# Splitting an expert's weights by halves over two engines in a two-block transformer kernel

## What is computed

```python
g_val, g_idx = lax.top_k(softmax(t @ w_group + b_group), 1)      # 1 of 4 groups
e_val, e_idx = lax.top_k(softmax(e_logits[group]), 2)            # 2 of its 8 experts
...
hid = silu(einsum('td,edf->tef', t, w1)) * einsum('td,edf->tef', t, w3)
hid = hid * combine[:, :, None]
y = einsum('tef,efd->td', hid, w2)
```

## Time and profile before

| what | value |
|---|---|
| median of 3 runs | 2845.2 us (2840.59 to 2852.76) |
| the profiled execution, its own time | 2848.42 us |
| its span, first to last instruction | 2846.7 us |
| busy: TensorE matmul, weight load | 90%, 70% |
| busy: VectorE, ScalarE, GpSimd | 62%, 34%, 53% |
| DMA moved | 386.72 MB, mean 136 GB/s |
| chain that ended last | TensorE 30%, GpSimd 20%, issue 19%, VectorE 14%, DMA 12%, ScalarE 3% |

### The profile page before, as it was taken

The page is one execution under the profiler, slowest core; times in us unless marked ns, Lnnn a source line. Parts: engine busy times, 40 slices in busy tenths (PEclk is TensorE's granted clock), DMA queues, the critical chain, the costliest instruction groups (busy, mean ns, idle before and its releaser), DMA issues.

```text
span 2846.7 us, 36510 instructions
## 1 busy us (share of the span) xinstructions
PE 2563.7 (90%) x12750; PEld 2006.6 (70%) x12750; DVE 1772.8 (62%) x2113; ACT 954.8 (34%) x1416; POOL 1515.9 (53%) x1234
## 2 busy tenths in 40 slices
PE   4977989968999999899598889999995879999998
PEld 3754767856777777678377348888884768888887
DVE  6769855647677776556688665666234964666314
ACT  2013256733443432567422222222013631222102
POOL 4730344526444453445366106767777847666775
PEclk8977889989999999899899679999997999999999
DMA  8746468952332322688522112333231113333222
GB/s 308 256 133 207 171 243 307 315 176 81 96 93 85 103 78 96 248 316 317 178 64 92 48 52 78 99 99 89 96 115 59 34 45 100 92 100 97 88 96 82
DMA packets 319121, 386.72 MB, mean 136 GB/s; under 512 B 51579, under 2 KB 259215, under 8 KB 318903
## 3 DMA queue, kind: packets, MB, share of 16 engines
q1 hardware_dynamic: 261424, 335.84, 35.8%
q10 hardware_dynamic: 34438, 28.08, 3.2%
q0 software_dynamic: 23168, 21.59, 2.4%
HBM read 397.62 MB, written 55.41 MB: 159 GB/s over the span
## 4 chain that ended last, share of the span: by engine, by line
PE 30%; POOL 20%; issue 19%; DVE 14%; DMA 12%; ACT 3%; SPq 1%; ACTq 0%; POOLq 0%; DVEq 0%
POOL WL L830 14%; PE PAIR L528 6%; PE PAIR L529 5%; PE PAIR L530 5%; POOL WH L826 5%; DMA RAW<-in_moe_w 4%; DMA RAW<-in_ffn_w_up 3%; PE PAIR L1831 2%; PE BANK L2261 2%; PE BANK L528 1%; PE BANK L529 1%; PE BANK L530 1%; DVE WL L1933 1%; DVE ADA_SUM L633 1%; PE PAIR L1801 1%
## 5 line engine op out<-in xcount | busy, mean ns | idle before, releaser
L830 POOL TENSOR_TENSOR WL<-RAW,WH 128x512 fp32r<-128x512 f32 x584 | 819.2, 1432 | 12.2
L528 PE MATMUL PAIR<-HH,WH 128*128 128x512 f32 x1792 | 713.2, 398 | 50.1 <-POOL HL L1119 29.1
L529 PE MATMUL PAIR<-HL,WH 128*128 128x512 f32 x1792 | 703.7, 393 | 0.0
L530 PE MATMUL PAIR<-HH,WL 128*128 128x512 f32 x1792 | 702.8, 392 | 0.0
L825 POOL TENSOR_TENSOR TURN<-ONES 128x1 f32<-128x1 f32 x146 | 34.3, 235 | 938.7 <-PE PAIR L530 860.5
L528 PEld LDWEIGHTS PAIR<-HH,WH 128*128 128x128 f32 x1792 | 340.3, 190 | 134.8 <-issue 45.7
L529 PEld LDWEIGHTS PAIR<-HL,WH 128*128 128x128 f32 x1792 | 340.4, 190 | 71.6 <-issue 2.4
L530 PEld LDWEIGHTS PAIR<-HH,WL 128*128 128x128 f32 x1792 | 340.1, 190 | 71.8
L826 POOL TENSOR_SCALAR WH<-RAW 128x2048 fp32r<-128x2048 f32 x146 | 281.5, 1928 | 0.0
L1933 DVE TENSOR_TENSOR WL<-RAW,WH 128x2048 fp32r<-128x2048 f32 x78 | 178.6, 2292 | 151.2 <-ACT WH L1751 135.7
L2003 POOL DMA_INDIRECT XG<-htok_scratch,GATHER_I x78 | 148.0, 1897 | 213.1 <-PE PAIR L1801 131.3
(11 more groups left out here) (523 smaller groups left out, 4649.2 us busy)
## 6 DMA issues: line engine op xcount, KB each, us to landing
RAW<-in_moe_w SPq DMA_DIRECT2D x156, 512.0 KB
RAW<-in_ffn_w_up SPq DMA_DIRECT2D x88, 512.0 KB
W2RAW<-in_moe_w SPq DMA_DIRECT2D x78, 512.0 KB
ADA_B<-in_ada_w SPq DMA_DIRECT2D x30, 1024.0 KB, 5.4
RAW<-in_ssm_w_in SPq DMA_DIRECT2D x48, 512.0 KB
ADA_A<-in_ada_w SPq DMA_DIRECT2D x18, 1024.0 KB, 7.7
RAW<-in_ffn_w_down SPq DMA_DIRECT2D x32, 512.0 KB
RAW<-in_ev_w_in SPq DMA_DIRECT2D x20, 512.0 KB
```

What stands on the lines that cost most here:

```text
L528: nc.tensor.matmul(o, wh, xh, start=start, stop=False)
L529: nc.tensor.matmul(o, wh, xl, start=False, stop=False)
L530: return nc.tensor.matmul(o, wl, xh, start=False, stop=stop)
L830: ins = pool.tensor_tensor(WL[:, s, c], RAW[:, s, c], WH[:, s, c].bitcast(F32), ALU.subtract)
```

## The change

A slot's unit is now handled in halves. w1 and w3 are loaded by two transfers with a semaphore each: w1 counts on the new `w1_landed`, w3 alone on `landed` (so the wait counts of all later units change: `landed_count`). ScalarE makes WH in two instructions of 1024 columns: the first when w1 has landed, signalling the new `w1_hi`, the second when w3 has landed, signalling `split_hi`. VectorE makes WL of the first half and signals the new `w1_low`. GpSimd makes WL of the second half in one instruction of 1024 columns (`second`) and signals `split_ready`. `second(0)` stands ahead of GpSimd's constants, `second(1)` behind `gather(1)`, and `second(s + 1)` between `gather(s + 2)` and `scatter(s - 3)` of each pass. SyncE waits for `w1_low` before it loads the first half of a buffer again, and for `split_ready` before the second half. TensorE's `up` waits for both.

```diff
+    moe_units = {plan.u[f"moe{layer}"] + s for layer in range(2) for s in range(SLOTS)}
+    def landed_count(u):
+        return sum(16 if v in moe_units else 32 for v in range(u % 2, u + 1, 2))
...
     def split_unit(pool, u, off=0):
-        pool.wait_ge(landed[s], off * 16 + 32 * (u // 2 + 1))
+        pool.wait_ge(landed[s], off * 16 + landed_count(u))
...
+    w1_landed = [sem("w1_landed0"), sem("w1_landed1")]
...
     def act_expert_high(act, layer, e, s):
         u = plan.u[f"moe{layer}"] + s
-        act.e.wait_ge(landed[u % 2], turns(e, 32) + 32 * (u // 2 + 1))
+        act.e.wait_ge(w1_landed[s % 2], turns(e, 16) + 16 * (slots_of(s % 2) * layer + s // 2 + 1))
         act.e.wait_ge(unit_done, turns(e, 2) + (u - 1))
-        act.e.activation(WH[:, u % 2], RAW[:, u % 2], ACT.Copy).then_inc(split_hi, 1)
+        act.e.activation(WH[:, u % 2, 0:D], RAW[:, u % 2, 0:D], ACT.Copy).then_inc(moe_sems["w1_hi"], 1)
+        act.e.wait_ge(landed[u % 2], turns(e, 16) + landed_count(u))
+        act.e.activation(WH[:, u % 2, D:], RAW[:, u % 2, D:], ACT.Copy).then_inc(split_hi, 1)
...
         (pe_moe, up)
+            pe.e.wait_ge(w["w1_low"], turns(e, 2) + (SLOTS * layer + s + 1))
             pe.e.wait_ge(split_ready, turns(e, 2) + (u + 1))
...
         (dve_moe, weights)
-            dve.e.wait_ge(split_hi, turns(e, 2) + (u + 1))
-            dve.e.tensor_tensor(WL[:, u % 2], RAW[:, u % 2], WH[:, u % 2].bitcast(F32), ALU.subtract).then_inc(split_ready, 1)
+            dve.e.wait_ge(w["w1_hi"], turns(e, 2) + (SLOTS * layer + s + 1))
+            dve.e.tensor_tensor(WL[:, u % 2, 0:D], RAW[:, u % 2, 0:D], WH[:, u % 2, 0:D].bitcast(F32), ALU.subtract).then_inc(w["w1_low"], 1)
...
         (pool_moe)
+        def second(s):
+            u = u0 + s
+            pool.e.wait_ge(split_hi, u + 1)
+            pool.e.tensor_tensor(WL[:, u % 2, D:], RAW[:, u % 2, D:], WH[:, u % 2, D:].bitcast(F32), ALU.subtract).then_inc(split_ready, 1)
+        second(0)
         pool.wait(total_ready)
...
         gather(0)
         gather(1)
+        second(1)
         for s in range(SLOTS):
             if s + 2 < SLOTS:
                 gather(s + 2)
+            if s and s + 1 < SLOTS:
+                second(s + 1)
             if s >= 3:
                 scatter(s - 3)
...
         (sp_moe, up)
-            load_unit(sp, part(0, w1), part(1, w3), off=i, u=u0 + s)
+            u = u0 + s
+            if s >= 2:
+                sp.wait_ge(w["w1_low"], i + (SLOTS * layer + s - 1))
+            else:
+                sp.wait_ge(split_ready, u - 1)
+            sp.dma_start(RAW[:, u % 2, 0:D], w1.rearrange("(p k) n -> p (k n)", k=KD)).then_inc(w1_landed[s % 2], 16)
+            if s >= 2:
+                sp.wait_ge(split_ready, i + (u - 1))
+            sp.dma_start(RAW[:, u % 2, D:], w3.rearrange("(p k) n -> p (k n)", k=KD)).then_inc(landed[u % 2], 16)
```

More of the change, by code:

```diff
@@ L1477, in build @@
     moe_sems = {s: sem(f"moe_{s}") for s in ("exp_in", "exp_out", "consts", "mask", "experts", "mapped", "index", "saved", "rows_hi", "silu",
-                                             "summed", "rows", "down", "combined", "shift",
+                                             "summed", "rows", "down", "combined", "shift", "w1_hi", "w1_low",
                                              "y_turned")}
@@ L1983, in pool_moe @@
     def pool_moe(pool, layer):
-        w = moe_sems
+        w, u0 = moe_sems, plan.u[f"moe{layer}"]
+        def second(s):
[3 more added lines that the diff above has]
+        second(0)
         pool.wait(total_ready)
@@ L2035, in up @@
             w1, w3 = weights_of(i, s, "moe_w1", "moe_w3")
-            part = lambda m, wm: (wm.rearrange("(p k) n -> p (k n)", k=KD), lambda raw: raw[:, m * D:m * D + D])
-            load_unit(sp, part(0, w1), part(1, w3), off=i, u=u0 + s)
+            u = u0 + s
[7 more added lines that the diff above has]
+            sp.dma_start(RAW[:, u % 2, D:], w3.rearrange("(p k) n -> p (k n)", k=KD)).then_inc(landed[u % 2], 16)
         def down(i, s):
```

## The result

The changed kernel takes 2893.57 us in the median of four runs (2889.82 to 2898.26), the kernel before 2847.22 beside it: a ratio of 1.0163, 95% interval 1.0145 to 1.0182. The prediction said 2864 us, slower; the direction was right, the loss more than twice as large as forecast.

The account below looks back on a forecast made before the run. Reloading RAW was taken to bound much of the loops, TensorE the rest; the late scatter would bind next. Loops +18.6, gathers -2.4, router +2.5 make +18.7 on 2848.4, 2867.1; 2864 us against the runs' median, range 2827 to 2912.

Parts of the forecast that it names:

- What bounds the loop before: Both expert stages: reloading the two-unit RAW buffer holds steps at 5.79 us mean, above TensorE's own 5.45.
- the ceiling of the loops: Both stages' loops: most that can be gained is the step time over TensorE's 5.45 us, 24.5 us or 0.9%.
- What is late next: Expert loops: the scatter, behind GpSimd's new part, makes ScalarE's OG copy wait; 6.08 us a step, +18.6 us over 64 slots.
- the fixed part of the loop: Two-slot loop through ScalarE's high parts, GpSimd's part, scatter and OG copy: 8.15 us for two steps, without the scatter's landing.
- The size of L: Time from the end of a scatter's issue to its landing: 4.0 us taken, between 1.1 and 6.4 or 7.2.
- its own formula: Expert loops: two steps take 8.15 us plus L, the scatter's landing time; 6.08 us a step at L 4.0.
- GpSimd's part: Low part of the second half, 1024 columns on GpSimd in each slot: 2.35 us, from between 2.3 and 2.6.
- A + 2.6: Expert loops: GpSimd's low part ends 2.6 us after A, the end of ScalarE's high part of unit s+1.
- The router: Ahead of each stage: second(0) on GpSimd delays VectorE's LOGIT + ROUTER_B, +1.7 us first stage, 0.8 second, sum +2.5.
- The start of the stages: gather(0) ends sooner because VectorE's low part beside it is half as long: -1.2 us in each stage, -2.4 in all.
- The one that ends faster, L under 2.3: Rival: scatter lands early, L 1.1 to 2.5, loops near TensorE's floor; 2821, more likely 2826 to 2835 us; chance 0.22.
- The one with an L as before, 5.5 to 6.4: Rival: scatter stays as slow as now, steps 6.8 to 7.3 us, 65 to 95 us more, 2905 to 2940; chance 0.18.

Follow-up runs that it names:

- the halves alone: Against the kernel before: loads and high parts in halves, VectorE makes both low halves, GpSimd's queue unchanged; 2826.9 us, ratio 0.9912; again 2824.9 us, 0.9920.
- the kernel of before with a wait only: Kernel before plus a GpSimd wait for VectorE's low part of unit s + 1, between gather(s + 2) and scatter(s - 3), computing nothing; 2926.8 us.

## Why the prediction was right or wrong

**What bounds the loop before** was right: the halves alone bring steps from 5.83 and 5.75 to 5.58 and 5.53, near TensorE's 5.45. That is 36 x (0.25 + 0.22) = 17 us of the 24.5 that were worked out as the ceiling of the loops. The whole time fell by 25 us, 0.9%, and that it equals the ceiling is chance: 5.0 us of it lie, by the profile, between the first gather and the first turn of the two stages, a stretch that moves from run to run.

**What is late next** was right, shown from both sides: moving the scatter removes the loss, and putting it behind a bare wait makes one. The place, the waiting instruction and the fixed part of the loop (8.0 us in the two steps shown, 8.15 worked out) held. The DMA share fell to 0.82 over 400 to 560 us, where 0.85 was forecast.

**The size of L** is the step that failed. The prediction took 4.0, "near the middle" between 1.1 and 7.2; the trace has 4.8. With 4.8 its own formula gives (8.15 + 4.8)/2 = 6.48 us, 0.69 above 5.79, and 64 x 0.69 = 44 us, where 18.6 stood. The measured 44.5 is that sum: over the 64 steps that the prediction counts the step grew by 0.66 and 0.73 us in the two stages. 0.8 us in one term, halved by the loop and taken 64 times, is 26 us. The relative error is large because only what L has beyond 3.4 us costs anything: 0.6 us by the forecast, 1.4 as measured. The L of 4.8 lies inside the forecast's own 3.5 to 5, but the range of time given for it, up to 2890 us, is too narrow: at L = 5 the formula gives 6.58 us a step, 64 x 0.79 = 50 us, so 2896 us. What was missing in the argument is a price for the queue in front. It named the loads of w3 and w1 and then took a value between two ends; the load of w2 it didn't name. In the changed kernel w2 is issued 2.6 us ahead of the scatter in the median, w1 2.0 and w3 0.14. Cutting w2 to an eighth takes 0.7 us off L and cutting w3 1.7, each in a loop that then runs faster, so these two are not prices that can be added up.

**GpSimd's part** was put at 2.35 us; it takes that in the two cases where VectorE does nothing beside it, and 2.49 in the mean, where it begins inside VectorE's last 0.3 us. Its end, A + 2.6, was right.

**The router** was right to a tenth: LOGIT + ROUTER_B went from 0.31 to 1.94 us in the first stage and 1.12 in the second, and the stretches from the LOGIT product to gather(0) grew by 1.67 and 0.83 us, against 1.7 and 0.8. For the second stage that was luck: the half was taken without a row. The Trainium skill (SBUF — State Buffer, Who interferes with whom) has the rule: a VectorE instruction with two SBUF inputs and a GpSimd one that reads SBUF shut each other out for the whole instruction. The trace agrees: the product that began at 335.13, inside GpSimd's part, ended at 337.07, 0.17 us after that part.

**The start of the stages** was put at -1.2 us each. gather(0) took 1.57 us in place of 2.65 in the earlier trace rows, 1.1 us less, as forecast:

```profile
357.23 2.36 DVE L1943 TENSOR_TENSOR WL<-RAW,WH 128x1024 fp32r<-128x1024 f32 x2
357.92 1.57 POOL L2019 DMA_INDIRECT XG<-htok_scratch,GATHER_I  x1 [18.63 <-DMA htok_scratch<-HTOK]
...
359.79 1.01 POOL L2019 DMA_INDIRECT XG<-htok_scratch,GATHER_I  x1 [0.31 <-issue]
```

But from gather(0) to the first turn it is 1.06 and 0.62 us less than before, and the kernel of before with a wait only, whose VectorE part is unchanged, shows 1.07 and 0.57 less. So the term is not shown to be there; at 2.4 us it would be small beside the 46 measured.

**The rivals.** The one that ends faster, L under 2.3, did not come; even with w3 nearly gone L was 3.0. The one with an L as before, 5.5 to 6.4, was the nearer neighbour: L fell from 6.1 to 4.8, but not to 4.0. That idler engines are what shortened it isn't shown, since the wait-only kernel has idler ones and an L of 5.6; what goes out just ahead of the scatter changed as well.

## What to carry to other kernels

An in-order queue that is given new work must be read for what stands behind it, DMAs above all: ask when each transfer issued there is next waited for, and subtract its flight. Put short issues whose operands are ready ahead of an instruction that waits. And where a forecast hangs on one latency near the value at which it begins to cost, multiply its possible error by the number of steps, and size it from the transfers that stand in front of it and not from the middle between two ends.

## What was not expected of the hardware

An indirect write of one slot's rows lands 1.1 us after its issue with nothing in front and 3.0 to 6.1 us in the mean of these loops. At a DMA share of 0.74 or 0.72 it was 4.1 or 3.0 us, according to which load was cut.

The gathers' issue on GpSimd got shorter by itself: 1.90 us in the mean before and 1.03 after. Two of the runs part the causes. With the low part in halves on VectorE and the gather where it was, it takes 1.37 us; with the whole low part and the gather behind a wait for it, 1.07. The rows of the kernel before show why: in its first stage 22 gathers begin inside VectorE's low part, and each ends 0.86 to 1.03 us after that part, whether it began early or late (1.75 to 3.07 us long); the other 17 take 0.99 to 1.01 us. The Trainium skill (SBUF — State Buffer, Who interferes with whom) says that a tensor_tensor of two SBUF inputs doesn't hold up descriptor generation, as an inference. The trace differs from the page.
